# First stage of a hybrid decoder layer: two dense units on two chunks, K tile by K tile, between the w_ada products

## The reference

```python
mod = jax.nn.silu(c) @ w_ada + b_ada                 # w_ada is 1024 x 6144
sh1, sc1, gt1, sh2, sc2, gt2 = jnp.split(mod[:, None, :], 6, axis=-1)
h = rmsnorm(x, norm1_g) * (1.0 + sc1) + sh1
proj = h @ w_in                                      # xr, gr, q, k, v, o, ig, fg, u
```

## Time and profile before

| what | value |
| --- | --- |
| time, median of three runs | 1196.27 us (1195.33 to 1197.08) |
| span of the profiled execution | 1193.2 us (its time outside the span is not recorded) |
| PE busy | 1144.6 us, 96% of the span |
| DVE, ACT, POOL busy | 705.4, 428.6, 305.6 us |
| DMA | 109.87 MB, mean 92 GB/s |
| chain that ended last | 81% PE, 10% DVE, 3% ACT, 3% DMA |

### The profile page before, as it was taken

How to read it: one execution, slowest core, us unless ns; L and a number is a source line. 1 busy time by engine, 2 the same in 40 slices (tenths; PEclk the granted TensorE clock), 3 DMA queues, 4 the chain that set the end, 5 groups by cost and what they waited for, 6 DMA issues and landing times.

```text
span 1193.2 us, 19528 instructions
## 1 busy us (share of the span) xinstructions
PE 1144.6 (96%) x7381; PEld 1096.3 (92%) x7381; DVE 705.4 (59%) x1253; ACT 428.6 (36%) x716; POOL 305.6 (26%) x263
## 2 busy tenths in 40 slices
PE   4899999999989999999999999999999999999997
PEld 1698888889879999899999999999999999999996
DVE  4561355688775344786655655655745656656646
ACT  5542365464554353641321321411321311412431
POOL 0431101110535366761210210210210210200352
PEclk9799999999989999999999999999999999999998
DMA  8813433667344712121121120120210211111104
GB/s 304 315 65 110 124 107 124 200 176 229 121 113 137 243 54 71 37 71 37 36 72 36 54 69 21 53 70 18 59 64 19 69 53 35 53 53 36 36 1 143
DMA packets 61702, 109.87 MB, mean 92 GB/s; under 512 B 6434, under 2 KB 30278, under 8 KB 61254
## 3 DMA queue, kind: packets, MB, share of 16 engines
q1 hardware_dynamic: 51430, 84.88, 21.5%
q10 hardware_dynamic: 10208, 24.12, 6.5%
HBM read 96.81 MB, written 12.18 MB: 91 GB/s over the span
## 4 chain that ended last, share of the span: by engine, by line
PE 81%; DVE 10%; ACT 3%; DMA 3%; issue 1%; POOL 1%; SPq 1%; POOLq 0%; DVEq 0%; ACTq 0%
PE D L2298 13%; PE D L2300 13%; PE D L2299 13%; PE D L2114 6%; PE D L2116 6%; PE D L2115 6%; PE X L2300 5%; PE X L2298 5%; PE X L2299 5%; DMA RAWW<-in_WADA 1%; PE X L2085 1%; PE X L2141 1%; PE X L2142 1%; PE X L2143 1%; PE X L2189 1%
## 5 line engine op out<-in xcount | busy, mean ns | idle before, releaser
L976 POOL TENSOR_TENSOR Y_lo<-FU,Y_hi 128x344 fp32r<-128x344 f32 (+2 forms) x120 | 123.8, 1036 | 556.4 <-ACT Y_hi L1116 554.9
L1832 DVE SCALAR_TENSOR_TENSOR X<-D,MOD,X 128x344 f32<-128x344 f32 (+1 forms) x216 | 123.8, 573 | 136.8 <-PE D L2300 113.8
L2298 PE MATMUL D<-Y_hi,W_hi 128*128 128x344 f32 x576 | 185.0, 321 | 0.0
L2299 PE MATMUL D<-Y_lo,W_hi 128*128 128x344 f32 x576 | 183.9, 319 | 0.0
L2300 PE MATMUL D<-Y_hi,W_lo 128*128 128x344 f32 x576 | 183.9, 319 | 0.0
L2114 PE MATMUL D<-H_hi,W_hi 128*128 128x344 f32 x472 | 157.9, 335 | 3.7 <-POOL H_lo L976 3.1
L2115 PE MATMUL D<-H_lo,W_hi 128*128 128x344 f32 x472 | 151.8, 322 | 0.0
L2116 PE MATMUL D<-H_hi,W_lo 128*128 128x344 f32 x472 | 151.8, 322 | 0.0
L2298 PEld LDWEIGHTS D<-Y_hi,W_hi 128*128 128x128 f32 x576 | 108.3, 188 | 1.2 <-issue 0.9
L2300 PEld LDWEIGHTS D<-Y_hi,W_lo 128*128 128x128 f32 x576 | 108.4, 188 | 0.0
L2299 PEld LDWEIGHTS D<-Y_lo,W_hi 128*128 128x128 f32 x576 | 108.1, 188 | 0.0
(11 more groups left out here) (358 smaller groups left out, 2658.0 us busy)
## 6 DMA issues: line engine op xcount, KB each, us to landing
RAWW<-in_W SPq DMA_DIRECT2D x76, 512.0 KB, 3.6
RAWW<-in_WADA ACTq DMA_DIRECT2D x28, 512.0 KB, 4.2
RAWW<-in_WADA SPq DMA_DIRECT2D x20, 512.0 KB, 8.0
RAWW<-in_W ACTq DMA_DIRECT2D x18, 512.0 KB, 3.7
X0T<-in_x SPq DMA_DIRECT2D x3, 1376.0 KB, 13.1
out_y<-OUTN SPq DMA_DIRECT2D x24, 172.0 KB
X<-in_x SPq DMA_DIRECT2D x8, 344.0 KB, 5.5
NM<-nm_d SPq DMA_DIRECT2D x8, 256.0 KB, 5.2
```

Source lines behind the costliest of these rows:

```text
L976: nc.gpsimd.tensor_tensor(lo_v, fu_v, hi_v.bitcast(F32), ALU.subtract).then_inc(lo_ready, 1)
L1832: tell(V.scalar_tensor_tensor(out=tile(X, m_x, a, a + w), in0=DB[bank][:, 0:w], scalar=tile(MOD, m_g, 0, 1), in1=tile(X, m_x, a, a + w), o ...
L2298: T.matmul(out, w_h, hi(kt), start=(kt == 0), stop=False)
L2299: T.matmul(out, w_h, lo(kt), start=False, stop=False)
```

## The change

MIX_ORDER's first part is written anew. ADT and ADM of a pair now stand right behind its product. Dense units 0 and 1 on chunks 0 and 1 (four accumulations) run in steps of one or two K tiles between the conditioning products, and N:1 is made between the pieces of N:0. V:0 comes after all four. The fourth accumulation, unit 1 on chunk 1, has the bank X1 (BESIDE), which V:0 uses next. All conditioning products use X4, all their ADT X3. DVE computes the rest of W:0 and W:1 in place of POOL (N_DVE_W). In the first norm DVE adds the shift from kt 4 on (SHIFTED_FIRST). SP_AFTER has another order.

```diff
-SP_AFTER = {3: ("x1",), 10: ("w1", "w0",), 16: ("wv",), 17: ("w2",), 18: ("x2",)}
+SP_AFTER = {3: ("x1",), 7: ("w0", "w1"), 15: ("wv", "x2"), 17: ("w2",)}
+N_DVE_W = 2
 MIX_ORDER = """
-ADA:0:0 ADA:0:1 SQ:0:0 ADA:4:0 ADA:4:1 SQ:0:1 SQ:1:0 ADT:0 ADM:0 ADA:1:0 SQ:1:1 ADA:1:1 ADT:4 ADM:4 NS:0
-ADA:5:0 ADA:5:1 N:0:0 ADT:1 ADM:1 N:0:1 ADA:2:0 ADA:2:1 ADT:5 ADM:5 ADA:6:0 ADA:6:1 ADT:2 ADM:2 N:0:2 ADA:3:0 W:0
-    ADA:3:1 ADT:6 N:0:3 W:1 ADM:6 ADA:7:0 ADA:7:1 ADT:3 N:0:4 N:0:5 ADM:3 ADT:7 ADM:7 N:0:6 N:0:7 NS:1
-DK:0:0:0:6
-WV:0 DK:1:0:0:6
-DK:0:0:6:8
-WV:1 WV:2 DK:1:0:6:8
-ADA:8:0
-D:0:0 WV:3
-D:1:0 N:1:0 N:1:1 N:1:2 N:1:3 N:1:4 V:0 SQ:2:0 DK:0:1:0:1
...
-D:0:1
-D:1:1 N:2:8 N:2:0 R:21 N:2:1 N:2:2 N:2:3 N:2:4 N:2:5 N:2:6 V:3 V:4 ADM:8 DK:0:2:0:8
-N:2:7 W:2 V:5
+ADA:0:0 ADA:0:1 SQ:0:0 ADT:0 ADM:0 ADA:4:0 ADA:4:1 SQ:0:1 ADT:4 ADM:4 NS:0
+SQ:1:0 ADA:1:0 ADA:1:1 N:0:0 N:0:1 ADT:1 ADM:1 SQ:1:1 ADA:5:0 ADA:5:1 W:0 ADT:5 ADM:5 NS:1 N:0:2 N:0:3 W:1
+ADA:2:0 ADA:2:1 DK:0:0:0:2 ADT:2 ADM:2 N:1:0 N:1:1 ADA:6:0 DK:1:0:0:2 ADA:6:1 DK:0:0:2:4 ADT:6 ADM:6 N:0:4 N:0:5 DK:1:0:2:4
+N:1:2 N:1:3 ADA:3:0 DK:0:1:0:1 DK:1:1:0:1 ADA:3:1 DK:0:1:1:2 DK:1:1:1:2 ADT:3 ADM:3 DK:0:0:4:6 ADA:7:0 DK:1:0:4:6 N:1:4 N:1:5
+    ADA:7:1 DK:0:1:2:3 DK:1:1:2:3 ADT:7 ADM:7 N:0:6 N:0:7 DK:0:1:3:4 DK:1:1:3:4 N:1:6 N:1:7
+WV:0 DK:0:0:6:8 DK:1:0:6:8
+D:0:0 WV:1 DK:0:1:4:6 DK:1:1:4:6
+D:1:0 WV:2 DK:0:1:6:8
+D:0:1 WV:3 DK:1:1:6:8
+D:1:1 SQ:2:0 V:0 SQ:2:1 ADA:8:0 R:20 V:1 ADA:8:1 NS:2 V:2 ADT:8 N:2:8 N:2:0 R:21 N:2:1 V:3 ADM:8 N:2:2 N:2:3 N:2:4 N:2:5 V:4 N:2:6
+N:2:7 DK:0:2:0:8 W:2 V:5
+BESIDE = (1, 1)
         elif k == "ADA" and s[2] == 0:
-            add(("ADA", s[1]), "X3" if s[1] in ADA_START[::2] else "X4")
+            add(("ADA", s[1]), "X4")
         elif k == "ADT":
-            add(s, "X1" if s[1] in ADA_START else "X4" if s[1] == NPAIR - 1 else "X3")
+            add(s, "X4" if s[1] == NPAIR - 1 else "X3")
-    SHIFTED = KT - 2
+    SHIFTED, SHIFTED_FIRST = KT - 2, KT // 2
-                if kt >= SHIFTED:
+                if kt >= (SHIFTED if shift else SHIFTED_FIRST):
+                elif k == "W" and s[1] < N_DVE_W:
+                    u = s[1]
+                    dve.wait_ge(w_hi_ready, u + 1)
+                    V.tensor_tensor(W_lo[:, u, :], WR[u][:], W_hi[:, u, :].bitcast(F32), ALU.subtract).then_inc(w_lo_ready, 1)
+                    if t == 0:
+                        d, n = dense_use(*BESIDE)
+                        pe.wait_ge(d_free[d], n + 1)
```

More of the change, by code:

```diff
@@ L995, in _ @@
                 if k == "W":
-                    if s[1] < N_EARLY_W:
+                    if s[1] < N_DVE_W:
+                        pass
+                    elif s[1] < N_EARLY_W:
                         w_lo(s[1], None, s[1] % 2, WR[s[1]])
@@ L1184, in _ @@
                     kind, t = UNIT_KIND[u]
-                    src = DB[d][:, 0:CH]
+                    src = (XB["X1"] if (u, c) == BESIDE else DB[d])[:, 0:CH]
                     samples = DB[d][:, LAST:CH]
@@ L2155, in _ @@
                     pe.wait_ge(w_lo_ready, u + 1)
-                    if n and k0 == 0:
+                    if n and k0 == 0 and (u, c) != BESIDE:
                         pe.wait_ge(d_free[d], n)
@@ L2159, in _ @@
                         pe.wait_ge(lo_ready, full_at[("N", c, kt)] + 1)
-                        dense(u % 2, c, H_hi, H_lo, d, kt, kt + 1)
+                        dense(u % 2, c, H_hi, H_lo, d, kt, kt + 1, XB["X1"] if (u, c) == BESIDE else None)
                 elif k == "G1":
```

## The result

| | before | after |
| --- | --- | --- |
| time, median | 1196.67 us (1195.33 to 1197.59, 4 runs) | 1204.66 us (1203.54 to 1206.55, 4 runs) |
| ratio | | 1.0061, 95% interval 1.0039 to 1.0084 |
| span of the profiled execution | 1193.2 us | 1202.3 us |
| V:0 starts | 55.50 | 70.32 |
| last K tile of DK:0:2 starts | 91.42 | 99.39 |

The kernel is 8.0 us slower. The profiled execution took 1204.06 us, 1.8 above its span.

A forecast was written before the change was run, and what follows sets the result against it. It took PE as the bound from 160 us and PE's waits on loads before about 45 us. DK:0:2 would end at 98.1 against 91.9: 1196.3 + 6.2, rounded down for later stages to 1202.3 us, range 1191 to 1207.

The forecast's parts named there:

- main case: Start to the end of DK:0:2: the schedule as priced, 6.2 us slower, likeliest 1199 to 1205 us; chance 0.48.
- rival A: Conditioning products: loads keep the pace, ADS copies don't bind PE, tile 15 lands at 37 to 38; 8 us faster, 1188; chance 0.20.
- Step 1: NS:0, no longer behind chunk 1's squares: reciprocal 22.05 to 24.4 us, before 26.21 to 28.5, a gain of 4.1 us.
- Steps 2 to 4: ADS copies of pairs 1, 5 and 2 behind squares, norm pieces and W:1 on ACT: done at 26.4, 31.8, 41.3 us.
- Step 5: Pairs 6, 3 and 7, upper clock level taken: copy of pair 3 to 52.9, of pair 7 to 57.0, ADM:7 58.5 us.
- Step 6: Tail from N:0:6 to N:1:7: DVE's pieces to 62.7 us, PE's last 12 K tiles to 67.6.
- The term for the port: Four shifts on DVE before V:0, contending with POOL: 0 to 0.43 us each, 0 to 1.7 in all; 0.5 taken.
- Step 7: Value weights: D:0:1 and WV:3 on ACT, then the rest on DVE; V:0 starts at 69.2 us.
- Step 8: V:0 to DK:0:2: DK:0:2 ends at 98.1 us behind the last H_lo, against 91.9, so 6.2 us later.
- Behind the mark: After the last K tile of DK:0:2: a later stage with its own chain can swallow up to 1 us.
- the costs put at nothing: Loads, banks X1 and X4, and W_lo on DVE beside ACT's copies: each costed at nothing.
- Rival C: PE's clock stays low until V:0: 1205 to 1207 us; chance 0.17.

## Why the prediction was right

It gave 1202.3 us, 1191 to 1207, and slower as the likeliest; the time was 1204.66, at the upper end of its main case (1199 to 1205). The main case was the right one, and rival A fell on its own point: tile 15 was issued near 46, not 38, and V:0 started near 70, not 54.

- Step 1: NS:0's reciprocal started at 21.55 (foreseen 22.05), a gain of 4.7 us over 26.21, where 4.1 stood.
- Steps 2 to 4: the copies of pairs 1, 5 and 2 ended at 25.76, 31.46 and 40.73; foreseen 26.4, 31.8, 41.3. The run with ACT's order alone shows that this chain is the cause; until then it was only argued.
- Step 5: ADT:3 started at 52.37, ADT:7 at 57.32; foreseen 52.9 and 57.5.
- Step 6 is where the size was off. It took the upper clock level to the end of the tail. The clock was up until about 62.3, then 12 matmuls had a pitch of 0.29 in place of 0.157 us: about 1.5 us up to the return to the upper level at 65.92. The two runs in which the clock stayed up give the same 1.5 from ADT:7 to V:0 (13.00 against 11.5). As the chain was still 0.2 us ahead at ADT:7, V:0 came 1.1 us after the 69.2 foreseen. The term for the port was not on the path: one shift of the four took 1.10 us, 0.7 more than its 0.40 and more than the 0.43 bounded for one, but H_lo of its piece was done by 64.64 and PE called for it only at 66.87.
- Step 7 was right as a chain: V:0 waited for the last rest of the value weights, behind D:0:1 and WV:3, and not for their load.
- Step 8: DK:0:2 ended at about 99.9 against 98.1: the 1.1 from before, and 0.7 more from there, most of it in the wait for the last H_lo. A shift that was held for 0.95 us in place of 0.40 (95.88 on DVE) stood ahead of that piece. That makes the mark 8.0 us later than before, not 6.2.
- Behind the mark the prediction let later stages give up to 1 us back; the profiled execution lost another 1.1 us there. Its waits for EX are 3.2 us, before 1.6. They are no part of the change: the kernel before with the new loads has 3.7 of them and a span of 1194.0. They differ from one execution to the next.
- Of the costs put at nothing, the loads and W_lo are none, each by a run of its own: with the old loads V:0 came 2.5 us later, and with W_lo on POOL ADT:2 came no earlier. The banks were tested in the kernel before alone, where the single bank cost 1.45 to 2.1 us at V:0; what it costs beside the late copies of the changed kernel is open.

Rival C had the mechanism that was missing, with another place: not low all the way to V:0, but low again near its end. The low stretch cost 1.5 us and not the 3 of the upper bound, and it is not part of every execution: in two of the five runs with the same wait the clock did not fall. Without it V:0 would have come near 68.8 (an estimate, 70.32 less 1.5), 0.4 us before the 69.2 foreseen. By the Trainium skill (TensorE: Matmul & The Clock Gate, HAM oscillation) a kernel that waits on a DMA between its K tiles lets the clock fall at each wait, and the next K tile starts at half speed. The trace agrees only in part: the wait was for POOL and not for a DMA, the first five matmuls behind it ran at the upper level, and behind the next wait (1.40 us at 70.32) it did not fall.

## What to carry to other kernels

Where work is put between the links of a chain that crosses engines (PE, ACT, PE), read the list once for each engine: a copy of 0.37 us behind squares and norm pieces that wait for DVE cost 3 us of PE, three times over. Put the links at the head of every queue and the filling behind them; with that the 24 matmuls in the gaps gained 3.3 us here, and without it the change lost 8. When two profiles differ by a microsecond or two, look first whether the clock took the same course in both. When one such wait is taken away, look at what is ready only just in time behind it (here the value weights, then DVE itself) before forecasting the whole gain.

## What I had not expected of the hardware

The granted clock fell in the midst of dense work. PE had waited 2.26 us for H_lo up to 61.13, the first five matmuls behind it ran at the upper level, and from 62.57 the pitch was 0.29 us until about 65.9, with PE busy all the time (2.00 of 2.00 us in both windows above). The waits of 1.40 us at 70.32 and 1.10 us at 98.53 were followed by no such fall in these rows (99.39 is the next K tile, its row 0.43 long, not 0.49). Nor does the same wait always do it. Five runs have 2.26 or 2.27 us of it at the same place. The clock fell behind it in the changed kernel, with the old loads (pitch 0.29 from 65.00) and with ACT's order alone (pitch 0.29 from the second matmul, at 55.66); it stayed up with W_lo on POOL and with the shifts on ACT. What decides it the rows don't show.

A shift on DVE that begins beside POOL's H_lo ended 0.2 us behind it in these rows, and so its length goes by where it falls: 1.10 us from 60.96 to 62.06, while POOL's two H_lo ran from 59.90 to 61.87, and 0.40 for the shift before it, which had begun 0.09 us before POOL did. DVE's timeline, then POOL's:

```profile
59.81 0.40 DVE L1533 TENSOR_SCALAR FU<-FU,MOD 128x344 f32<-128x344 f32 x1
...
60.96 1.10 DVE L1533 TENSOR_SCALAR FU<-FU,MOD 128x344 f32<-128x344 f32 x1
```

```profile
59.90 1.97 POOL L960 TENSOR_TENSOR H_lo<-FU,H_hi 128x344 fp32r<-128x344 f32 x2 [3.08 <-ACT H_hi L1102]
```
